# Feed-forward stage: split weights kept in DRAM after the first token group, loaded back by POOL's queue, and five rotating product banks

## The reference

```python
h = _rmsnorm(x, g_pre_ffn) * (1.0 + sc_f) + sh_f
gate, up = jnp.split(jnp.einsum('btd,df->btf', h, w_ffn_in), 2, axis=-1)   # 1024 -> 2 x 2816
f = jnp.einsum('btf,fd->btd', jax.nn.silu(gate) * up, w_ffn_out)           # 2816 -> 1024
x = x + gt_f * _rmsnorm(f, g_post_ffn)
```

## Time and profile before

| | us |
|---|---|
| median of 3 runs | 2886.8 |
| lowest, highest | 2883.4, 2894.22 |
| the profiled execution | 2890.9 |
| its span, first to last instruction | 2888.8 |
| granted TensorE clock, mean over the span | 0.955 |

### The profile page before, as it was taken

One profiled execution on the slowest core, in us unless ns is written; L12 is line 12 of the kernel. 1 busy time (PEld: TensorE's weight loads), 2 busy tenths in 40 slices (PEclk: granted clock), 3 DMA queues, 4 the chain that ended last, 5 costly groups with the idle time before them and its releaser, 6 DMA issues. The chain is left out here.

```text
span 2888.8 us, 42580 instructions
## 1 busy us (share of the span) xinstructions
PE 2571.6 (89%) x15492; PEld 2394.7 (83%) x15492; DVE 2006.8 (69%) x2686; ACT 1289.4 (45%) x2228; POOL 1280.2 (44%) x741
## 2 busy tenths in 40 slices
PE   5999999758888959996899999779999977999995
PEld 2999999747777747774799999779999977999995
DVE  2597789657767746744677777787777778777776
ACT  3456545347777754453433333343333334333333
POOL 1575567222323211001666556546655654665561
PEclk8999999979999979997999999889999998999997
DMA  5355445253333236964132222134222213322222
GB/s 213 121 176 168 130 142 173 71 135 84 90 98 94 60 99 196 278 184 122 59 127 73 80 67 88 44 103 147 74 81 67 88 44 102 108 74 80 67 74 85
DMA packets 199097, 315.37 MB, mean 109 GB/s; under 512 B 18210, under 2 KB 156194, under 8 KB 189938
## 3 DMA queue, kind: packets, MB, share of 16 engines
q1 hardware_dynamic: 174578, 295.80, 32.4%
q10 hardware_dynamic: 24320, 16.87, 2.2%
HBM read 266.29 MB, written 46.37 MB: 108 GB/s over the span
## 5 line engine op out<-in xcount | busy, mean ns | idle before, releaser
L2030 POOL TENSOR_TENSOR p_c_lo<-p_graw,p_c_hi 128x512 fp32r<-128x512 f32 x198 | 296.4, 1504 | 265.9 <-ACT p_c_hi L2138 265.9
L2030 POOL TENSOR_TENSOR p_c_lo<-ffn_wraw,p_c_hi 128x512 fp32r<-128x512 f32 x198 | 275.6, 1403 | 293.7 <-ACT p_c_hi L2138 293.7
L328 POOL TENSOR_TENSOR p_w_lo<-p_wraw,p_w_hi 128x1024 fp32r<-128x1024 f32 x100 | 295.6, 2966 | 211.9 <-ACT p_w_hi L389 211.7
L2112 PE MATMUL p_y<-p_f_hi,p_o_hi 128*128 128x342 f32 (+1 forms) x1056 | 341.5, 323 | 14.2 <-POOL p_o_lo L2035 14.2
L2112 PE MATMUL p_y<-p_f_lo,p_o_hi 128*128 128x342 f32 (+1 forms) x1056 | 340.0, 322 | 0.0
L2112 PE MATMUL p_y<-p_f_hi,p_o_lo 128*128 128x342 f32 (+1 forms) x1056 | 339.5, 322 | 0.0
L2355 DVE TENSOR_TENSOR p_y<-p_y 128x342 f32<-128x342 f32 (+1 forms) x480 | 234.3, 507 | 99.5 <-PE p_y L2112 99.5
L349 PE MATMUL p_proj<-p_h_hi,p_w_hi 128*128 128x412 f32 (+1 forms) x800 | 285.1, 356 | 15.5 <-POOL p_w_lo L328 15.2
L349 PE MATMUL p_proj<-p_h_lo,p_w_hi 128*128 128x412 f32 (+1 forms) x800 | 280.2, 350 | 0.0
L349 PE MATMUL p_proj<-p_h_hi,p_w_lo 128*128 128x412 f32 (+1 forms) x800 | 280.2, 350 | 0.0
L2138 ACT ACTIVATE p_c_hi<-p_graw 128x512 fp32r<-128x512 f32 x198 | 119.9, 621 | 341.1 <-DVE p_graw L2292 239.8
(11 more groups left out here) (313 smaller groups left out, 7098.7 us busy)
## 6 DMA issues: line engine op xcount, KB each, us to landing
p_wraw<-w_in SPq DMA_DIRECT2D x100, 512.0 KB, 4.8
p_graw<-w_ffn SPq DMA_DIRECT2D x33, 1024.0 KB, 5.0
ffn_wraw<-w_ffn SPq DMA_DIRECT2D x65, 512.0 KB, 3.6
ffn_wraw<-w_ffn SPq DMA_DIRECT2D x32, 1024.0 KB, 5.3
p_ada<-w_ada SPq DMA_DIRECT2D x32, 512.0 KB, 4.4
z<-p_zout SPq DMA_DIRECT2D x48, 206.0 KB, 2.8
p_ada_ring<-w_ada SPq DMA_DIRECT2D x4, 2048.0 KB, 21.7
p_mix<-mix SPq DMA_DIRECT2D x16, 512.0 KB, 6.1
```

The costliest lines, as they stand in the source:

```text
L328: pool.tensor_tensor(w_lo[s][:], wraw[:, s, :], w_hi[s][:].bitcast(F32), ALU.subtract).then_inc(lo_done, 1)
L2030: pool.tensor_tensor(c_lo[r][:], source(p), c_hi[r][:].bitcast(F32), ALU.subtract).then_inc(S["lo"], 1)
L2112: mm = pe.matmul(Y[q % YB][:, 0:W], a[s][:, m, :], b[s][:, n, 0:W], start=s == 0 and i == 0, stop=s == 1 and i == 2)
```

## The change

Four parts in `ffn`, and a renaming of semaphores in the stage before it.

1. **Weights are combined and split once.** `s_add`, `high_w`, `high_o` and POOL's subtractions run in units 0 to 21 only. The hi and the lo part of a product's weights are now one buffer `c[r]` (128 x 2 x 4 x 128, 512 KB), those of `o` one of 1 MB. In group 0 SP stores each of them to DRAM (`w_parts`, `o_parts`) once its low part is made, with at most two stores in flight; a buffer is written again only after its store has landed. In groups 1 and 2 POOL does no arithmetic: its queue loads `c[r]` once product p - 6 is done, and the two `o` buffers of a pair in the odd unit.
2. **Banks.** Products use five banks in rotation (`Z[p % 5]`), tiles three instead of four. A product waits for the last reader of product p - 5: for j = 0 to 6 that is c11, u2 and t of the unit before, then c21 and c12 of the unit before, then the copy of product 0 (`first_product`) and u4 of its own unit.
3. **Order at turns, ends and tail.** `low_t` 2 and 4 go from POOL to DVE at the two turns (not in unit 0), and DVE's list is rearranged: c11 comes before t3, u2, t, c22 and u4 before t2, and `low_t` 5 and 6 wait for the next unit. At the ends `gate` of half 0 is done a unit earlier, the sums on PE stand behind products 2 and 4, and the parts of half 1 move forward. In the tail the last `output` of half 0 is POOL's, and `root` of half 0 stands before `gate` of half 1. The loads of x wait for the sum on PE instead of for `tree`.
4. **`o` splits in group 0** are made one in every unit, at its start, instead of two in the odd units.

```diff
-YB = 4
+YB = 3
+ZB = 5
@@ POOL @@
             def low_w(p):
-                if p < NPR * NU4:
+                if p < NPR * FT:
                     r = p % NR
-                    pool.wait_ge(S["hi"], p + 1)
-                    pool.tensor_tensor(c_lo[r][:], source(p), c_hi[r][:].bitcast(F32), ALU.subtract
+                    wait_hi(pool, "c", p)
+                    pool.tensor_tensor(c[r][:, 1], source(p), c[r][:, 0].bitcast(F32), ALU.subtract).then_inc(S["lo"], 1)
+                elif p < NPR * NU4:
+                    r, q = p % NR, p % (NPR * FT)
+                    wait_prod(pool, p - NR)
+                    if p - NR < NPR * FT:
+                        wait_store(pool, "c", p - NR)
+                    if p < 2 * NPR * FT:
+                        wait_store(pool, "c", q)
+                    pool.dma_start(c[r][:], io["w_parts"][q // NPR, q % NPR]).then_inc(c_in[r], 16)
+
+            def low_o(u):
+                if u < FT:
+                    wait_hi(pool, "o", u)
+                    pool.tensor_tensor(o[u % 2][:, 1], oraw, o[u % 2][:, 0].bitcast(F32), ALU.subtract
                                        ).then_inc(S["lo"], 1)
+                elif u < NU4:
+                    wait_tile(pool, done[u - 2])
+                    ...
+                    pool.dma_start(o[u % 2][:], io["o_parts"][u % FT]).then_inc(o_part[u % 2], 16)
...
             for u in range(NU4):
-                if u % 2:
+                if u and (u <= FT or u % 2):
                     low_o(u - 1)
                 low_w(NPR * u + 5)
                 low_w(NPR * u + 6)
                 low_w(NPR * (u + 1))
                 low_w(NPR * (u + 1) + 1)
-                if turn:
-                    low_t(turn, 2)
+                if u % 2 and u >= FT:
+                    low_o(u)
                 low_w(NPR * (u + 1) + 2)
                 low_w(NPR * (u + 1) + 3)
-                if turn:
-                    low_t(turn, 4)
                 low_w(NPR * (u + 1) + 4)
-                if u % 2:
-                    low_o(u)
+            output(NGR - 1, 0)
@@ SP @@
+            def store(kind, i):
+                k = STORE[kind, i]
+                if k >= 2:
+                    sp.wait_ge(stored[k % 2], 16 * (k // 2))
+                wait_lo(sp, kind, i)
+                if kind == "c":
+                    sp.dma_start(io["w_parts"][i // NPR, i % NPR], c[i % NR][:].bitcast(F32)).then_inc(stored[k % 2], 16)
+                else:
+                    sp.dma_start(io["o_parts"][i], o[i % 2][:].bitcast(F32)).then_inc(stored[k % 2], 16)
@@ PE, product(p) @@
-                out = (A, Dk, B, C, A, B, C)[j]
-                pe.wait_ge(S["lo"], p + 1)
+                out = Z[p % ZB]
+                if u < FT:
+                    wait_lo(pe, "c", p)
+                else:
+                    wait_c(pe, p)
...
-                if j < 4:
-                    wait_comb(pe, u - 1, ("t", "u4", "c21", "c12")[j])
-                if j == 4:
-                    pe.wait_ge(S["p1"], u + 1)
-                if j == 5:
-                    wait_comb(pe, u, "c11")
-                if j == 6:
-                    wait_comb(pe, u, "u2")
+                if p >= ZB:
+                    v, i = (p - ZB) // NPR, (p - ZB) % NPR
+                    if i == 0:
+                        wait_unit(pe, "p1", 0, v)
                     else:
+                        wait_comb(pe, v, (None, "u4", "c11", "u2", "t", "c21", "c12")[i])
@@ ACT @@
             def high_w(p):
-                if p < NPR * NU4:
+                if p < NPR * FT:
                     u, j = p // NPR, p % NPR
-                    wait_prod(act, p - NR)
+                    if p >= NR:
+                        wait_prod(act, p - NR)
+                        wait_store(act, "c", p - NR)
@@ DVE, the new order of a unit @@
                 if u:
                     comb(u - 1, "c12"); collect(u - 1, 6); gated(u - 1, 1)
                 if ends is not None: tree(ends, 0)
                 collect(u, 0)
                 if u: low_f(u - 1, 1)
                 s_add(u, "s4")
                 if turn: low_t(turn, 0); t_add(turn, "t1")
                 if G and t == 0: low_t(G, 5)
                 if ends is not None: tree(ends, 1)
                 if late is not None: output(late, 1)
                 collect(u, 1); s_add(u + 1, "s3")
                 if G and t == 0: low_t(G, 6)
                 collect(u, 2); comb(u, "c11")
                 if turn: low_t(turn, 1); t_add(turn, "t3")
                 s_add(u + 1, "s1"); comb(u, "u2")
                 if ends is not None: inverse(ends, 0); scale(ends, 0)
                 collect(u, 3); comb(u, "t"); comb(u, "c22"); comb(u, "u4")
                 if turn: t_add(turn, "t2"); low_t(turn, 2)
                 if ends is not None: output(ends, 0)
                 collect(u, 4); s_add(u + 1, "s2"); comb(u, "c21"); gated(u, 0)
                 if turn: low_t(turn, 3); t_add(turn, "t4")
                 collect(u, 5); low_f(u, 0)
                 if turn: low_t(turn, 4)
                 if ends is not None: inverse(ends, 1); scale(ends, 1)
```

More of the change, by code:

```diff
@@ L2223, in _ @@
                     high_t(G, 6)
-                if G and t == 1:
-                    squares(G - 1, 1)
-                if G and t == 2:
-                    root(G - 1, 1)
+                if ends is not None:
+                    squares(ends, 1)
                 first_product(u)
@@ L2240, in _ @@
                     high_t(0, 5)
-                if G and t == 1:
-                    gate(G - 1, 0)
                 silu(u, 0)
+                if ends is not None:
+                    root(ends, 0)
+                    gate(ends, 1)
                 high_w(NPR * (u + 1) + 1)
@@ L2256, in _ @@
                     high_t(turn, 4)
-                if u % 2:
-                    high_o(u)
+                if ends is not None:
+                    root(ends, 1)
                 high_f(u, 0)
                 high_w(NPR * (u + 1) + 4)
-                if G and t == 1:
-                    gate(G - 1, 1)
                 if turn:
@@ L2266, in _ @@
                     squares(G - 1, 0)
+                    gate(G - 1, 0)
             silu(NU4 - 1, 1)
+            high_o(NU4 - 1)
             high_f(NU4 - 1, 1)
-            for n in range(2):
-                squares(NGR - 1, n)
-                gate(NGR - 1, n)
-            for n in range(2):
-                root(NGR - 1, n)
+            squares(NGR - 1, 0)
+            gate(NGR - 1, 0)
+            squares(NGR - 1, 1)
+            root(NGR - 1, 0)
+            gate(NGR - 1, 1)
+            root(NGR - 1, 1)
         @block.vector
@@ L2437, in _ @@
                     gated(u - 1, 1)
-                if G and t == 0:
-                    low_t(G, 6)
                 if ends is not None:
                     tree(ends, 0)
-                if late is not None:
-                    inverse(late, 1)
                 collect(u, 0)
@@ L2478, in _ @@
                 comb(u, "u4")
+                if turn:
+                    t_add(turn, "t2")
+                    low_t(turn, 2)
+                if u == 0:
+                    low_t(0, 6)
                 if ends is not None:
[L2480 removed]
+                    output(ends, 0)
                 collect(u, 4)
                 s_add(u + 1, "s2")
[L2483 to L2484 removed]
                 comb(u, "c21")
                 gated(u, 0)
[L2487 to L2488 removed]
+                if turn:
+                    low_t(turn, 3)
+                    t_add(turn, "t4")
                 collect(u, 5)
@@ L2491, in _ @@
                 if turn:
-                    low_t(turn, 5)
+                    low_t(turn, 4)
                 if ends is not None:
-                    output(ends, 0)
+                    inverse(ends, 1)
+                    scale(ends, 1)
             comb(NU4 - 1, "c12")
```

307 lines of the change are left out of this document (179 added, 128 removed).

## The result

| | us |
|---|---|
| before, median of 4 runs on the same chip | 2885.98 (2883.4 to 2894.22) |
| changed, median of 4 runs | 2848.44 (2845.11 to 2860.87) |
| ratio | 0.9873, 95% interval 0.9836 to 0.991 |
| changed, the profiled execution and its span | 2851.48, 2849.7 |

A forecast was written before the change was run, and what follows sets the result against it. PE, busy 89% of the span, bounds the kernel, with losses to recover at turns, ends and tail. 2890.9 - 37.5 - 2 - 2 + 2.5 + 2 = 2853.9 us; the median lies 4.1 lower, so 2850; range 2828 to 2905.

The forecast's parts named there:

- case (a): Whole kernel: the forecast holds with all bounds near the values taken, 2830 to 2870 us, chance 0.60.
- The transfers (part 1): Steady units: new stores land in 4 to 4.5 us and loads come in time, both at cost 0.
- the signs that I had named for being wrong: PE waiting for `c` or `o` loads, ACT's copies for stores, stores landing after over 5 us, product 6 visibly for u4.
- Rival (c): Group 0: stores bound it from a landing time of 5.0 us; 5.7 would give 2910 us; chance 0.18.
- rival (b): Groups 1 and 2: POOL's loads late by rate, issue time or lock, 2872 us at the bound or 2920; chance 0.12.
- the lock of rival (b): GpSimd's descriptor writing locked out by DVE's shared port use: loads start up to 1.58 us later, covered by the lead.
- Turns and ends: Changes of group: gains of 10 us at turn 1, 13.5 at turn 2, 7 at each end, together 37.5.
- The loads of x: At the ends: issued 20 us before use, so cost 0.
- Banks: Product 6's new wait for u4 costs 0.08 us in 33 odd units, 2.5 us; bounds 0 and 10.
- Tail: Behind the last tile: earlier root 0 and output on POOL end it 0.8 to 4.7 us earlier; 2 taken.
- Start: Unit 0: product 5's 1.8 us wait for c11 goes, gain 2 us.
- Late `o` splits: Even units of group 0: the later split costs 0.2 us in 11 units, 2 us; bounds 0 and 16.

The follow-up runs named there:

- e5: Changed kernel with one store in flight in place of two: 2967.51 us.
- e11: Changed kernel with POOL's weight loads issued when product p - 4 is done in place of p - 6: 2903.94 us.
- e12: Changed kernel with queues swapped, SP loading `c` and `o`, POOL transferring h2, x1 and y: 2854.44 us, ratio 0.9881.
- e4: Changed kernel with both `o` splits of a pair again around the odd unit in group 0: 2846.95 us, ratio 0.9857.
- e3: Changed kernel with the old four product and four tile banks and their waits: 2852.63 us, ratio 0.9872.
- e1: Kernel before with only the banks changed, five for products and three for tiles: 2897.7 us, ratio 1.0028.
- e9: Kernel before with caching alone (stores, loads, no splitting in groups 1 and 2), its banks and nearly all its order kept: 2836.51 us, ratio 0.982.
- e2: Changed kernel without caching, weights split in all groups, new order and banks kept: 2917.22 us, ratio 1.0102.
- e13: e10 with T_lo 2 and 4 on VectorE, its list in the order PE wants, transfers of x and y spread: 2822.07 us, ratio 0.9768.
- e6: Changed kernel with u4 and the sums before it ahead of T_lo 1, t3 and t2 at the turns: 2849.95 us, ratio 0.9871.
- e10: Caching alone in the kernel before, four product banks, with a new order for turns, ends and tail: 2838.51 us, ratio 0.983.
- e7: Changed kernel with t, c22, u4 before inverse 0 and scale 0 at the ends, output 0 in the next unit: 2843.02 us, ratio 0.9849.

## Why the prediction was right, and where it was not

Forecast 2850.0 us, measured 2848.44; case (a). Step by step:

**The transfers (part 1).** I took 4 to 4.5 us for the landing of a store and cost 0; the median is 4.3 us, and PE never waited for a store, nor for a load of weights. That the store has the load's shape and is not like x's store (5.7 us) was the right row to lean on. Two of the signs that I had named for being wrong did show: single stores landed after up to 12.3 us, and ACT's copies waited for stores 7 times in group 0, 18.8 us in all, up to 7.1 us. No wait of PE came of it, so the signs were drawn too narrowly. Rival (c) is a real edge, by e5: with one store in flight group 0 becomes 119 us longer. For rival (b), e11 shows the edge at a lead between three and five products; the lock of rival (b) shows nowhere (e12). A slip stands in the estimate beside rival (c): its figure lies 19% over the 301 GB/s, and 16% is the share of that figure.

**Turns and ends.** Predicted idle at turn 1 about 7 and 3 us, found 6.2 and 3.1; at turn 2 2.9 and 3.1, found 2.8 and 3.4 (starts of neighbouring matmuls less a step); at the ends 12.5 us in three pieces, found 10.5 and 10.3 (5.6, 4.0, 0.8 and 5.2, 4.2, 0.8 against 6.3, 1.6, 4.6). In the table units 21 to 25 gained 18.1 us (predicted 10 + 7) and 43 to 47 22.5 (13.5 + 7). The method, an old list's durations replayed in the new list, held within 1 us at the turns. There the second piece of turn 1 has another releaser than I had: PE waits 3.1 us for POOL's split of `o` at the first tile of unit 22, not for VectorE's collect at the fourth. The chain that I had worked out is there too, since e4 takes POOL's away and 3.1 us for the collect appear; that both give the same size is luck. At the ends the method did not hold, since the second piece is 2.4 us longer and the third 3.8 us shorter than I had.

**The loads of x, a term that I had put at nothing.** The prediction charges 0 for them, "issued 20 us before use". In the changed kernel both are issued from 1882.3 us on, output 0 could start at 1893.9, and the load has not landed: VectorE stands 4.2 us here and 4.7 at the second end, and c12 and PE's product 4 come later by it.

```profile
1898.01 3.09 DVE L2508 TENSOR_TENSOR p_E<-p_E,p_y 128x1376 f32<-128x1376 f32 x2 [4.16 <-DMA p_E<-x]
```

The loads of `c` and `o` fill the DMA beside them. First the landings from 1880 to 1900 us in the kernel before, then those in the changed kernel, then its busy time by stretch (the last columns as above):

```profile
p_E<-x SPq DMA_DIRECT2D x2, 1376.0 KB, 7.5
```

```profile
p_E<-x SPq DMA_DIRECT2D x2, 1376.0 KB, 16.6
```

```profile
1880.00:1890.00 10.00, 8.52 (x51) 7.83 (x49) 7.96 (x10) 5.73 (x11) 3.16 (x6) 1.00 1.07 388
```

I had worked out the new transfers' rate for steady units and not for the ends, where x comes on top. That the ends still gave 9.8 and 9.4 us (units 23 and 24, 45 and 46), more than the 7 forecast for each, is luck in this term: c12 came 3.2 us later than forecast and the first collect only 1.4, so that PE, held up before, found VectorE nearly ready at the fourth tile.

**The small terms.** Banks: 0.08 us an odd unit, by e3. Tail: 2.2 us instead of 2; POOL's output took 5.94 us (I had 6.5) and did hold up VectorE's scale 1, the case that I had put at 0.8. Start: predicted 2, found 0: of the waits of 1.8 us (c11) and 1.9 us (T_lo) in unit 0 one of 3.2 is left, and product 2's wait for POOL's split grew from 1.7 to 3.2. Late `o` splits: predicted 0.2 in 11 even units; 0.33 to 0.36 in each of 9, and units 3 to 21 grew by 4.3 us in all. PE's timeline at one of them:

```profile
1462.02 0.40 PE L2200 MATMUL p_y<-p_f_hi,p_o 128*128 128x344 f32 x1 [0.21 <-POOL p_o L2113]
```

Not foreseen: the steady units of groups 1 and 2 became 1.8 and 0.9 us shorter. Before, an even unit there takes 28.5 us and with caching 28.3: in the kernel before, the first tile's fourth matmul starts 0.15 us behind the end of POOL's split of `o`, some 0.2 us late, and in unit 40 0.9 us late. So "in steady units PE never waited" was nearly true, not quite. Against the forecast, turns and ends gave 3 us more and the steady units of groups 1 and 2 4 us more, the start 2 less and units 3 to 21 1.5 less. The errors partly cancel, and that 2850.0 came within 2 us of 2848.44 owes something to it.

**What was wrong is the account of the gain.** The prediction says, of the steady units, that taking work from VectorE, ACT and POOL "is worth nothing by itself". At the turns it does count the removed work, in t1's 1.58 us and the missing sums, but it gives it no price of its own and works out the whole gain from the rebuilt list; and it credits the banks with the longest wait, 9.0 us, "as such", which by e1 only moved to u4. The number came out, since a rebuilt list contains both effects. But e9 shows that the removal alone gives 52 us under the old order, and e2 that the rebuilt list without it loses 1%. By the table the order, the banks and the place of the `o` splits together cost 11 us against caching alone: 4.6 in units 3 to 21 (e4: the `o` splits), 3.9 and 2.2 at the two changes of group, 1.4 in the steady units of groups 1 and 2 (e3: the banks) and 1.0 at the two edges, against 2.1 won in the tail. To replay the old list with the new durations too could have shown it, and it is the replay that I left out.

Open: why the four banks lose in unit 22 what they win in unit 21 was not tried by itself, and the parts of e13 (T_lo on VectorE, order, spread transfers) were run only together. What e9 gives is not divided among shorter instructions of VectorE, its shorter list and POOL's missing splits.

## What to carry to other kernels

When a change removes work and reorders what is left, replay the old order without the work as well: here the removal was worth 52 us and the reordering, with it, minus 12; without the removal the same reordering cost 28 (e2), so the two are not a sum. Work on an engine with slack is not free where it slows its neighbour's instructions in a chain that sets the end. And when one wait is taken out by a new order, look at once at what stands behind it (e6: 3.8 us off u4, 4.5 on POOL; e10: the loads; e7 and e13: transfers of y and tokens), since the list of waits names only the one that came last. And when transfers are added, look for the stretch where others already run, and not only at the mean.

## What the runs showed that was not expected

- VectorE's f_lo of 128x342 takes 1261 ns on average in the steady state beside POOL's subtractions, and 514 ns without them.
- The landing time of a 512 KB transfer goes with what runs beside it: 2.7 us for a store alone, 4.3 with two in flight; 4.8 us for a load with three products of lead, 5.6 with five, 9.1 where the DMA is full. A load of x (1376 KB) lands after 7.5 us before and after 16.6 beside the new loads.
- One core moved 394 GB/s over 10 us, at a DMA share of 1.09. The Trainium skill ("Perfetto Trace Analysis", "Roofline") says that a single active core can pull more than the 358 GB/s that the prediction names beside rival (c), up to about 120% of it; the trace agrees. So 358 was no bound for these transfers, and the stores and loads of units 1 to 20 ran at 309 GB/s over 420 us (1395 to 1815) without a wait of PE for them.
